# Four gate tiles run in the last decode step ahead of its value products, and the output weights are asked for behind the last value pages

## What is computed

```python
def merge(h, oa, ob, w_gate, w_out_a, w_out_b, w_out):
    g = jax.nn.sigmoid((h @ w_gate).astype(F32)).astype(h.dtype)
    ga, gb = jnp.split(g, 2, axis=-1)
    return (ga * (oa @ w_out_a) + gb * (ob @ w_out_b)) @ w_out
```

## Time and profile before

| | |
|---|---|
| median of 3 runs | 739.8 us (736.12 to 740.52) |
| the profiled execution's own time | 738.92 us |
| its span, first to last instruction | 737.2 us |
| TensorE busy | 626.4 us (85%) |
| VectorE busy | 377.5 us (51%) |
| ScalarE busy | 197.6 us (27%) |
| mean granted TensorE clock | 0.932 |

### The profile page before, as it was taken

One profiled execution on the slowest core, in us unless ns is written; L12 is line 12 of the kernel. 1 busy time (PEld: TensorE's weight loads), 2 busy tenths in 40 slices (PEclk: granted clock), 3 DMA queues, 4 the chain that ended last, 5 costly groups with the idle time before them and its releaser, 6 DMA issues.

```text
span 737.2 us, 10914 instructions
## 1 busy us (share of the span) xinstructions
PE 626.4 (85%) x3894; PEld 500.8 (68%) x3894; DVE 377.5 (51%) x802; ACT 197.6 (27%) x458; POOL 84.7 (11%) x212
## 2 busy tenths in 40 slices
PE   2569999879787878989088996999999997999993
PEld 1369999645544645655056774999999996777772
DVE  0373862378476676775027306588887876100004
ACT  1344342423122122123210013345434441000111
POOL 0050000511112112111000000302111211200000
PEclk9869999999899899889589998899999999999996
DMA  5678874969989898992903333355335422233401
GB/s 167 196 100 252 325 227 155 324 249 355 366 307 322 305 356 291 329 378 84 393 1 115 114 115 108 124 165 187 121 123 195 155 81 80 82 104 132 156 0 64
DMA packets 96827, 141.96 MB, mean 193 GB/s; under 512 B 7629, under 2 KB 53521, under 8 KB 96788
## 3 DMA queue, kind: packets, MB, share of 16 engines
q1 hardware_dynamic: 42308, 73.55, 30.3%
q10 hardware_dynamic: 51968, 63.97, 25.7%
q0 software_dynamic: 2512, 3.95, 1.6%
HBM read 135.14 MB, written 6.30 MB: 192 GB/s over the span
## 4 chain that ended last, share of the span: by engine, by line
PE 70%; DVE 18%; DMA 3%; ACT 3%; SPq 2%; issue 2%; ACTq 1%; POOL 0%; DVEq 0%; POOLq 0%
PE ps L532 24%; PE ps L553 11%; PE ps L555 10%; PE ps L554 10%; DVE arena_k L1136 7%; PE ps L670 4%; SPq L385 2%; PE ps L525 2%; PE ps L785 1%; DMA arena_v<-in_cache_diff_v 1%; PE ps L705 1%; DMA wbuf<-in_w_up 1%; DVE hT L1126 1%; DVE arena_s L1341 1%; PE ps L714 1%
## 5 line engine op out<-in xcount | busy, mean ns | idle before, releaser
L553 PE MATMUL ps<-xhi,whi 128*128 128x288 f32 x352 | 107.1, 304 | 4.7 <-POOL xlo L445 4.7
L554 PE MATMUL ps<-xlo,whi 128*128 128x288 f32 x352 | 104.7, 298 | 0.0
L555 PE MATMUL ps<-xhi,wlo 128*128 128x288 f32 x352 | 104.4, 297 | 0.0
L532 PE MATMUL ps<-arena_q,wbuf 128*128 128x288 f32 x352 | 87.3, 412 | 4.2 <-DVEq L1434 4.2
L532 PEld LDWEIGHTS ps<-arena_q,wbuf 128*128 128x128 f32 x352 | 67.9, 193 | 23.5 <-DVEq L1434 4.5
L1136 DVE STREAM_TRANSPOSE arena_k<-arena_k 128x1024 f32<-128x1024 f32 x64 | 74.3, 1211 | 3.5 <-DMA arena_k<-in_cache_diff_k 3.5
L532 PE MATMUL ps<-hT,wbuf 128*128 128x288 f32 x256 | 75.1, 453 | 0.5 <-ACT arena_q L922 0.5
L553 PEld LDWEIGHTS ps<-xhi,whi 128*128 128x128 f32 x352 | 66.7, 189 | 6.1 <-issue 4.7
L553 PE MATMUL ps<-xhi,phi 128*128 128x288 f32 x192 | 58.2, 303 | 13.5 <-DVE plo L1141 13.5
L555 PEld LDWEIGHTS ps<-xhi,wlo 128*128 128x128 f32 x352 | 67.1, 191 | 0.0
L554 PEld LDWEIGHTS ps<-xlo,whi 128*128 128x128 f32 x352 | 67.1, 191 | 0.0
(11 more groups left out here) (194 smaller groups left out, 894.5 us busy)
## 6 DMA issues: line engine op xcount, KB each, us to landing
wbuf<-in_w_up ACTq DMA_DIRECT2D x22, 1024.0 KB, 7.6
arena_k<-in_cache_moba_k SPq DMA_DIRECT2D x64, 256.0 KB, 5.2
arena_k<-in_cache_diff_k SPq DMA_DIRECT2D x64, 256.0 KB, 6.0
arena_v<-in_cache_moba_v SPq DMA_DIRECT2D x64, 256.0 KB, 5.0
arena_v<-in_cache_diff_v SPq DMA_DIRECT2D x64, 256.0 KB, 6.4
wbuf<-in_w_in ACTq DMA_DIRECT2D x6, 2048.0 KB, 11.5
wbuf<-in_w_down ACTq DMA_DIRECT2D x8, 1408.0 KB, 6.2
wbuf<-in_w_gate ACTq DMA_DIRECT2D x8, 1024.0 KB, 8.9
```

Of the source, the lines that this page charges most:

```text
L532: last = mm(ps[:, bank, 0:TOK], w, x, start=(opens and k == 0), stop=(stop and k == len(moving) - 1))
L553: mm(ps[:, q, 0:TOK], high[:, q, k, :], xhi[:, k, :], start=(k == 0), stop=False)
L554: mm(ps[:, q, 0:TOK], high[:, q, k, :], xlo[:, k, :], start=False, stop=False)
L555: last = mm(ps[:, q, 0:TOK], low[:, q, k, :], xhi[:, k, :], start=False, stop=(k == DT - 1))
```

## The change

Which tiles run at which place is now a table. `p_gate` takes u and runs the tiles of `GATES[u]`: steps 1, 3, 4 and 5 lose the tile at their end (u = 6, 10, 12, 14), and tiles 12 to 15 run at u = 17, which is in step 7 ahead of the sum of the exponents and the value products. The gate loads are asked for by a second table, `GATE_LOAD`: load 5 at the end of step 2, load 6 in the middle of step 5, load 7 at the end of step 6. `w_oa` is asked for behind tile 13, whose load was the last in slot 0, and `w_ob` at the end of step 7. Each tile of the four still waits for the copy of the one ahead of it, as all use bank 7. A constant that nothing used goes.

```diff
@@ -301,7 +301,9 @@
-        HALVES = 16 + 4
+        GATES = {0: (0,), 1: (1,), 2: (2,), 3: (3,), 4: (4,), 5: (5,), 7: (6,), 8: (7,), 9: (8,), 11: (9,), 13: (10,),
+                 15: (11,), 17: (12, 13, 14, 15)}
+        GATE_LOAD = {1: 2, 3: 3, 5: 4, 8: 5, 13: 6, 16: 7}
@@ -647,11 +649,11 @@
-            def p_gate(m):
-
-                if m == 0:
+            def p_gate(u):
+
+                if u == 0:
                     pe.wait_ge(q_copied, 2)
-                if m < 16:
+                for m in GATES.get(u, ()):
                     pe.wait_ge(w_in[m // 2 % 2], W_GATE + 16 * (m // 4 + 1))
                     pe.wait_ge(in_taken, 4 + T_GATE + m)
                     tile(7, [slot_gate(m // 2 % 2)[:, k, m % 2 * P:m % 2 * P + P] for k in range(DT)], h
@@ -931,13 +933,16 @@
-            def p_gate(m):
-
-                if m < 16:
+            def p_gate(u):
+
+                for m in GATES.get(u, ()):
                     act.wait_ge(tile_ready, T_GATE + m + 1)
                     take_gate(PLACE[m], 7)
-                    if m % 2 == 1 and m // 2 + 2 < 8:
-                        load_gates(m // 2 + 2, m // 2 % 2)
+                    if m == 13:
+                        act.wait_ge(p_biased, 32)
+                        load(0, slot4(0), w_oa_v)
+                if u in GATE_LOAD:
+                    load_gates(GATE_LOAD[u], GATE_LOAD[u] % 2)
@@ -979,9 +984,7 @@
                 p_gate(u + 1)
-                if b == 6:
-                    act.wait_ge(p_biased, 32)
-                    load(0, slot4(0), w_oa_v)
+                if b == LAST:
                     load(1, slot4(1), w_ob_v)
```

## The result

The changed kernel takes 741.13 us (median; 739.04 to 746.91), the kernel before beside it on the same chips 738.44 us (734.51 to 740.52). The ratio is 1.0039, with a 95% interval of 1.0024 to 1.0054: some 2.9 us longer, between 1.8 and 4.0. That lies inside the range and inside the 1% called no change, but the interval is clear of no change, and the sign is not the forecast's: I had -0.6 us. The profiled execution took 741.54 us with a span of 739.8, against 738.92 and 737.2, so the two profiles differ by 2.6 us and can stand for the medians. The mean granted clock went from 0.932 to 0.926.

What follows compares the result with a forecast made beforehand. It took the last step to be bound by late value pages and earlier steps by VectorE's key turns. Terms -4.4 - 1.5 + 5.3 = -0.6 us gave 739.2 us against the median of 739.8; range 733.5 to 744.

Steps and rivals of the forecast that it cites:

- The last step: Step 7: four gate tiles fill TensorE's wait for value pages, and the value products return to 3.64 us; -4.4 us.
- The value pages no longer last: Step 7: with less loaded ahead, the pages land 14.2 us after 346.5, at about 361, before the four tiles end.
- The weights and gate loads: Steps 2 to 7 and projection: the moved gate loads and later output weights land in time and cost nothing.
- Tiles hidden in steps 1 and 3: Step ends: removing tiles hidden behind key turns gains nothing in steps 1 and 3, 0.75 us each in 4 and 5; -1.5.
- The cold keys: Ends of steps 1, 3, 4, 5: keys' products start at half clock after idling, 1.33 us each, +5.3; bounds 0 and 3.66.
- that of 159.80: Place in the trace before: 4.00 us idle, then keys' products took 4.99 instead of 3.66 us; source of the 1.33 price.
- the tiles in the middle of the steps only change their numbers: Middle of the decode steps: the gate tiles there are only renumbered; no time was entered in the sum.
- the clock holds: Rival: the small product keeps full clock in each idle stretch, keys stay at 3.66 us; -5.9, 733.9 us; chance 0.12.
- The keys cold to their end: Rival: keys' products run wholly at half clock, up to 3.66 us more each; +8.7, 748.5 us; slower past 1.5 each; chance 0.13.
- the tile at 297.55: Step 4's end tile before the change, read as half clock over all 6.55 us; evidence for keys staying cold.
- The pages coming last: Rival, step 7: the first output weight slows the last value pages past 367.3; losing all 2.1 us gives 741.3; chance 0.10.

Runs made afterwards that it cites:

- the experiment with two banks: The kernel with the middle tiles of steps 1 to 4 taken out, with tiles 13 and 15 in bank 5 instead of bank 7: 721.06 us, 0.9757.
- the filled kernel: The changed kernel plus eight unread products of a constant at each of the four ends that lost their tile: 732.5 us, 0.9919 of before.
- the fillers behind steps 1 and 3: The changed kernel with eight unread filler products only at the ends of steps 1 and 3: 738.73 us, 0.9996 of before; run again, 738.48 us.
- the shortened tiles: The kernel before with one product instead of eight in tiles 6, 10, 12 and 14, nothing moved: 746.76 us, 1.0106.
- the fillers behind 4 and 5: The changed kernel with eight unread filler products only at the ends of steps 4 and 5: 736.98 us, 0.9983 of before.
- the two kernels that move loads alone: The kernel before, both output weights asked for behind the last value pages: 730.62 us; or the first in mid step 6, only the second behind them: 731.74 us.
- fewer tiles moved: The kernel before with only the middle tiles of steps 1 and 3 taken out and two tiles in the last step: 725.16 us, 0.9819.

## Why the prediction was right and wrong, step by step

**The last step: right.** Forecast -4.4, measured -4.67. From the end of the last small product to the value products it is 18.03 us (356.29 to 374.32; forecast 17.9 and 0.32), before 20.37, so -2.34 against -2.1; the value products gained the other 2.34. The hand-over of 0.58 us was put together rightly from two places of the trace, and the experiment with two banks took it away.

**The value pages no longer last: right.** They do not appear in the chain. The last one is asked for at 361.0 and lands 8.2 us later, at about 369.2, some 5 us ahead of the value products at 374.32. That is 15.5 us behind the first request (353.74), where the forecast had 14.2; the rate of 370 GB/s was near (369 to 393 GB/s in each microsecond from 355 to 368). With two tiles fewer in the way the pages did come last (the wait of 3.15 us).

**The weights and gate loads: free, right.** No wait of the projection for a weight stands in the timeline after; the filled kernel has them at the same places and no longer step.

**Tiles hidden in steps 1 and 3, worth 0.75 us each in steps 4 and 5: right.** Steps 4 and 5 without their keys are 1.03 and 0.81 us shorter, 1.84 against 1.5, and the timeline gives VectorE's turns as what ends the waits. Of the last 0.3 us, 0.2 lie in step 4: before, VectorE waited 0.20 us for the small products at half the clock (1.97 us, 1.26 after), and after it does not wait there.

**The cold keys: mechanism right, price too small. This is the first of the two steps that failed: "The idle stretches of the change are longer than that of 159.80, so I take its price, 1.33."** The sentence names the reason why the row was a low one and then takes the row. The four places cost 1.28, 2.63, 1.88 and 1.36, together 7.15 instead of 5.3 us, 1.79 in the mean. A price is half of the time from the first product to the return of the clock, and one row gives one such time. Nor is this row steady. At the same place, behind the same 4.00 us of idle time, the same products took between 4.92 and 6.51 us in the 13 profiles; these two are of one kernel, the one with the fillers behind steps 1 and 3:

```profile
158.68 6.51 PE L672 MATMUL ps<-arena_k,arena_s 128*32 128x256 f32 x64 [4.01 <-DVE arena_k L1143]
```

```profile
159.38 5.09 PE L672 MATMUL ps<-arena_k,arena_s 128*32 128x256 f32 x64 [4.01 <-DVE arena_k L1143]
```

So 1.33 was one draw out of 1.26 to 2.85. The two bounds, nothing and 3.66, were both in the text, and so was the point from which the sign turns, 1.5 us; their middle, 1.83, would have been nearer than the row.

**"[...] the tiles in the middle of the steps only change their numbers": wrong for step 2, and the second step that failed.** Its middle tile took 5.41 us, 4.04 before, the rest of the step 0.28 more; step 3 is 0.30 longer. Together 1.95 us that the sum had at nothing and gave no reason for; this alone, as the cold keys' 1.85 alone, turns the sign of -0.6. In the four profiles with cold keys behind step 1 (the changed kernel twice, the shortened tiles, the fillers behind 4 and 5) this tile took 5.41 to 5.44. Where these keys were warm it took 4.04 in five profiles (before, the two kernels that move loads alone, all fillers, the second profile of the fillers behind 1 and 3), and 5.73 and 5.94 in two (the first profile of those fillers, and fewer tiles moved). So it came with the cold keys each time, but the clock can fall there without them, and why it does is not settled.

**The rest.** 1.85 and 1.95 us too much, 0.34 and 0.27 too little, make the +3.2 between -0.6 and the profiles' 2.6. The projection (-1.69) and the part behind it (+1.7) were not in the sum and cancel. The first came and went between executions of one kernel; for the second I have no experiment, and over the 13 profiles that part lasts 320.1 to 322.1 us.

**The rivals.** That the clock holds was refuted for the change itself, but the filled kernel is this rival made real: 732.5 us, where I gave 733.9. Its agreement is partly luck, as the fillers keep the 1.5 us that the rival counted as saved and the projection gave 1.7 instead. The keys cold to their end was right on the side and wrong on the size: no place was cold to the end, but two of four passed the 1.5 us, and so did the mean. Its row was misread: the tile at 297.55 was at half the clock until 302.5, 5 of its 6.55 us. The pages coming last did not happen.

## What to carry to other kernels

A hidden piece of work ahead of a burst may be what holds TensorE's clock up, or what goes through a slow stretch in the burst's stead, so ask of each instruction to be moved not only who waits for it but what runs right behind its place, and price that burst by its bounds instead of one row. Choose the pieces to move by who waits for them: here the tiles in the middle of the steps gained 2.2% by the same scheme with which the tiles at the ends lost 0.4%. And ask whether a smaller edit has the whole gain: the order of two loads alone gave 1.2%.

## What the hardware showed that I had not expected

- 28 products fewer made the kernel 8 us longer (746.76 against 738.72), and 32 products that nobody reads made another 8.6 us shorter.
- The same idle stretch of 5.50 us was followed by keys of 6.29 us in one place and 5.02 in another, and each place that was left empty kept its price within 0.04 us in the profiles of three kernels (the changed one twice, the shortened tiles, the fillers behind 4 and 5). With fillers at the two places ahead the later two changed theirs, and the place at 159.80, ahead of all edits, has another price from profile to profile.
- Sixteen pages of 256 KB alone took 14.7 us from the first request (347.18) to the last landing (361.87). The mean of 285 GB/s over that stretch is no rate to plan with: in between the transfers ran at up to 404 GB/s, and at both ends nearly nothing moved.
- A bank shared between a tile and the copy of the tile ahead of it leaves TensorE idle for 0.58 us at each hand-over; with two banks four tiles take 15.73 instead of 18.19 us, 0.82 for each of the three.
